# Turning the gathered rows of the experts as fp32r in place of fp32

## The reference

```python
logits = (xt @ w_router + b_router).astype(jnp.float32)
top_vals, top_idx = lax.top_k(logits, TOP_K)
top_gates = jax.nn.softmax(top_vals, axis=-1)
...
def expert_block(args):
    xb, e = args                       # up to 128 gathered tokens of expert e
    gate = xb @ w_gate[e] + b_gate[e]
    up = xb @ w_up[e] + b_up[e]
    gate = jnp.minimum(gate, SWIGLU_LIMIT)
    up = jnp.clip(up, -SWIGLU_LIMIT, SWIGLU_LIMIT)
    glu = gate * jax.nn.sigmoid(SWIGLU_ALPHA * gate)
    return (glu * (up + 1.0)) @ w_down[e] + b_down[e]
```

## Time and profile before

| | |
|---|---|
| median of 3 runs | 1856.83 us (1856.76, 1856.83, 1863.29) |
| profiled execution | 1863.21 us, span 1861.9 us |
| PE busy | 1802.1 us (97%) |
| DVE busy | 1421.6 us (76%) |
| ACT busy | 1177.9 us (63%) |
| POOL busy | 192.2 us (10%) |
| read from HBM | 481.56 MB |

### The profile page before, as it was taken

One profiled execution on the slowest core, in us unless ns is written; L12 is line 12 of the kernel. 1 busy time (PEld: TensorE's weight loads), 2 busy tenths in 40 slices (PEclk: granted clock), 3 DMA queues, 4 the chain that ended last, 5 costly groups with the idle time before them and its releaser, 6 DMA issues.

```text
span 1861.9 us, 20805 instructions
## 1 busy us (share of the span) xinstructions
PE 1802.1 (97%) x8267; PEld 1445.1 (78%) x8267; DVE 1421.6 (76%) x1219; ACT 1177.9 (63%) x879; POOL 192.2 (10%) x127
## 2 busy tenths in 40 slices
PE   7999969999999999999999999999998999999998
PEld 5777757888888888888888888888874777778876
DVE  4476569999999999999999999999895523765342
ACT  4353457777777777777777777777772346564231
POOL 1311010111211211111121121111001000000000
PEclk9999979999999999999999999999998999999999
DMA  7311339999999999999999999999995322122221
GB/s 259 114 46 68 130 142 360 368 367 364 362 379 365 359 381 361 368 363 367 365 366 371 367 360 370 365 369 369 367 360 216 136 68 68 46 73 90 94 77 45
DMA packets 95330, 487.16 MB, mean 262 GB/s; under 512 B 13864, under 2 KB 15440, under 8 KB 45312
## 3 DMA queue, kind: packets, MB, share of 16 engines
q1 hardware_dynamic: 81408, 462.64, 66.3%
q0 software_dynamic: 9520, 17.13, 2.4%
q10 hardware_dynamic: 4304, 6.03, 1.0%
HBM read 481.56 MB, written 20.97 MB: 270 GB/s over the span
## 4 chain that ended last, share of the span: by engine, by line
PE 93%; DVE 4%; ACT 2%; DMA 1%; issue 1%; SPq 0%; ACTq 0%; POOLq 0%; DVEq 0%
PE PS L445 85%; PE PS L677 3%; PE PS L849 1%; DVE WL L1229 1%; PE PS L861 1%; PE PS L842 1%; DMA ring<-in_w_in_dram 1%; ACT WH L914 1%; PE PS L477 0%; PE PS L555 0%; DVE X L1240 0%; DVE X L1552 0%; DMA xg<-h2d,tok 0%; DVE X L1555 0%; DVE HG L1559 0%
## 5 line engine op out<-in xcount | busy, mean ns | idle before, releaser
L1229 DVE TENSOR_TENSOR WL<-ring,WH 128x2048 fp32r<-128x2048 f32 x428 | 967.1, 2287 | 236.5 <-ACT WH L914 232.8
L914 ACT ACTIVATE WH<-ring 128x2048 fp32r<-128x2048 f32 x428 | 815.7, 1915 | 355.1 <-PE PS L445 350.4
L445 PE MATMUL PS<-WH,xh 128*128 128x512 f32 x1024 | 328.6, 402 | 4.1 <-ACT xh L1060 2.2
L445 PE MATMUL PS<-WL,xh 128*128 128x512 f32 x1024 | 317.6, 391 | 0.0
L445 PE MATMUL PS<-WH,xl 128*128 128x512 f32 x1024 | 274.5, 390 | 0.0
L445 PEld LDWEIGHTS PS<-WL,xh 128*128 128x128 f32 x1024 | 192.8, 188 | 41.2
L445 PEld LDWEIGHTS PS<-WH,xl 128*128 128x128 f32 x1024 | 192.7, 188 | 41.3
L445 PEld LDWEIGHTS PS<-WH,xh 128*128 128x128 f32 x1024 | 188.5, 189 | 43.5 <-ACT xh L1060 2.8
L1777 POOL DMA_INDIRECT yd<-ys,dst x32 | 74.0, 2314 | 971.2 <-ACT ys L1075 971.2
L445 PE MATMUL PS<-WH,hh 128*128 128x512 f32 x512 | 160.7, 395 | 1.1 <-ACT hh L1060 1.1
L445 PE MATMUL PS<-WL,hh 128*128 128x512 f32 x512 | 158.4, 390 | 0.0
(11 more groups left out here) (343 smaller groups left out, 2158.5 us busy)
## 6 DMA issues: line engine op xcount, KB each, us to landing
ring<-in_w_gate_dram SPq DMA_DIRECT2D x128, 1024.0 KB, 7.5
ring<-in_w_up_dram SPq DMA_DIRECT2D x128, 1024.0 KB, 7.3
ring<-in_w_down_dram SPq DMA_DIRECT2D x128, 1024.0 KB, 8.5
ring<-in_w_in_dram SPq DMA_DIRECT2D x32, 1024.0 KB, 5.4
ring<-in_w_out_dram SPq DMA_DIRECT2D x8, 1024.0 KB, 5.0
yk<-yd SPq DMA_DIRECT2D x4, 1024.0 KB, 9.3
X<-in_x_dram SPq DMA_DIRECT2D x4, 512.0 KB, 9.7
h2d<-HV ACTq DMA_DIRECT2D x4, 512.0 KB, 3.2
```

The source lines that it names most:

```text
L445: return P.matmul(ps, a, b, start=start, stop=stop)
L914: A.activation(WH[buf[n]], ring[spot[n]], ACT.Copy).then_inc(s_hi, 1)
L1229: V.tensor_tensor(WL[buf[n]], ring[spot[n]], WH[buf[n]].bitcast(F32), SUB).then_inc(s_lo, 1)
```

## The change

The two buffers xg get the type fp32r. A new tile identr of 128x128 fp32r holds the identity; DVE fills it once, by a copy of ident, in vector_routing. tensor_turn8 takes the type and the identity as arguments: for the gathered rows PE gets fp32r data, identity and output, for eu it stays fp32. GpSimd's gather and memset go to the same bytes as before through a cast of the type.

```diff
-    xg = [reg(f"xg{i}", [128, D], F32, 4 * i) for i in range(2)]
+    xg = [reg(f"xg{i}", [128, D], F32R, 4 * i) for i in range(2)]
+    identr = reg("identr", [128, 128], F32R, 49)
...
-    def tensor_turn8(src):
+    def tensor_turn8(src, dt, one):
         pairs_ = src.rearrange("t (c p k) -> t c k p", p=128, k=2)
         for k in range(8):
-            last = P.transpose(PS[:, 6 + k // 4, 128 * (k % 4):128 * (k % 4) + 128], pairs_[:, k // 2, k % 2], ident)
+            last = P.transpose(PS[:, 6 + k // 4, 128 * (k % 4):128 * (k % 4) + 128].bitcast(dt), pairs_[:, k // 2, k % 2], one)
         last.then_inc(s_tt, 1)
...
-        tensor_turn8(xg[e % 2])
+        tensor_turn8(xg[e % 2], F32R, identr)
...
-        tensor_turn8(eu.rearrange("p h f -> p (h f)"))
+        tensor_turn8(eu.rearrange("p h f -> p (h f)"), F32, ident)
...
         normed(HV[3], 3, 7, G2).then_inc(s_norm, 1)
+        V.tensor_copy(identr, ident)
         low(first + NS - 1)
...
-        G.indirect_dma_start(xg[i], None, h2d, bass.IndirectOffsetOnAxis(tok[:, e:e + 1], 0), bounds_check=T - 1,
+        G.indirect_dma_start(xg[i].bitcast(F32), None, h2d, bass.IndirectOffsetOnAxis(tok[:, e:e + 1], 0), bounds_check=T - 1,
...
-            G.memset(xg[i], 0.0).then_inc(s_mz, 1)
+            G.memset(xg[i].bitcast(F32), 0.0).then_inc(s_mz, 1)
```

## The result

The changed kernel takes 1860.54 us in the median of 22 runs (1859.45 to 1866.54), the kernel before 1857.94 us (1856.22 to 1863.29, 22 runs). The ratio is 1.0019 with a 95% interval of 1.0012 to 1.0025: slower by 3.5 us (2.2 to 4.6; the two medians alone are 2.6 us apart, and the runs of either kernel spread over 7 us). That is under the 0.5% that I had called no change, but it is clear of noise and on the other side of zero than my sum of -0.3 us. The time lies inside my range of 1851 to 1866 us, but by luck: the room above was left for the slower of two levels of the same program, not for a dearer transpose.

What follows compares the result with a forecast made beforehand. PE was taken to bound the kernel; 256 transposes at 119 against 120 ns gave -0.3 us, the other terms 0, so 1856.83 - 0.3 = 1856.5 us, with a range of 1851 to 1866 us.

Steps and rivals of the forecast that it cites:

- the room above: Upper end of the 1851 to 1866 us range, added for the upper of one program's two levels, 1856.8 and 1863.3.
- What bounds the kernel: PE sets the pace, busy 1000.00 of 1000.00 us from 300 to 1300 us; transfers follow at 367 GB/s.
- the sum for the 256 transposes: PE's turns of gathered rows: a rounded transpose costs 119 ns against 120 in fp32, together -0.3 us.
- both bounds: Limits for the 256 transposes: -2.3 us if fp32r removes the step's penalty, +1.5 us from a product batch at 126 ns.
- The lower bound from the step: Turns of xg: fp32r might remove the penalty for taking every second element, 256 x -9 = -2.3 us.
- The load rule of the Trainium skill: PE's weight loads: 107 ns for 128 columns, so at most 13 ns gained per transpose, -3.3 us, more likely nothing.
- Rival 1: Rounded transposes of gathered rows are paced by their columns, 67 ns not 120: -13.6 us, 1843.2 us; chance 11%.
- Rival 3: Each rounded transpose runs as an ordinary single precision product in two halves, 275 ns: +39.7 us, 1896.5 us; chance 6%.
- Rival 2: Transposes get faster but the weights do not follow, DMA staying at 367 GB/s: about 1856 us, no change; chance 3%.
- The copy on DVE: In the routing after HV, the 128x128 identity copy, nearest row 0.22 us, fits into a 0.89 us wait: 0.
- GpSimd's work and the remainder xl: GpSimd's memset, gather and casts move the same bytes; DVE's xl and its products keep size and time: no cost.
- The first turn: First turn of gathered rows at 250.33 us, 1.98 us at a low clock: costed at nothing, at most half given back.

Runs made afterwards that it cites:

- The probes: Kernel before plus series of 16 PE instructions behind its last product; with a step of two: fp32 transposes 115 to 120 ns, fp32r transposes 141, fp32r products 118 to 121.

## Why the prediction was wrong

**What bounds the kernel: right.** A change of a turn's price came through to the whole. The thirty turns give 0.13 us per expert and the kernel lost 3.5 us, with both turns rounded it lost twice that, and PE stayed busy for all of the 1000 us from 300 to 1300. Of the 4.0 us between my 1856.5 and the measured 1860.54, 1.1 us is only that the median of the kernel before went from 1856.83 to 1857.94 with more runs.

**The step that failed** is the sum for the 256 transposes, "119 against 120 ns, 256 x -1 = -0.3 us". The 119 ns were measured on ordinary fp32r products, and for those they are right: with the same rows and step as the change an ordinary product kept the kernel at 0.9994, and its probe gives 118 ns. I carried the number over to a transpose on the ground that the load of 128 four-byte columns sets the pace in either. That is what the runs refute: a rounded transpose costs 81 to 88 ns side by side, less than any product, and 140 with a step of two, more than any other form with that step. The transposes inside a turn went from 120 to 140 ns, and net of the earlier start of the turn (0.13 us per turn of eight) the term is 256 x about +16 ns, +4.2 us, outside both bounds (-2.3 to +1.5 us), since both bounds came from products and from fp32.

**The lower bound from the step pointed the wrong way.** I had seen that fp32 loads pay for a step (111 against 120 ns) and asked only what it would be worth if fp32r did away with it. That fp32r could pay more for it was not asked. That the time still fell inside the range of 1851 to 1866 us is luck. The step was in front of me, as xg's load row of 205 ns beside HG's of 144.

**The load rule of the Trainium skill** ("TensorE: Matmul & The Clock Gate", section on LDWEIGHTS: the columns over 1.2, with no term for the type, so 107 ns for 128) fits the fp32 transposes and fp32r products that read neighbours (109 to 113 ns). The rounded transpose differs from it both ways, 81 to 88 ns and 140, and so does the product with a step of four, 234 ns; the measurement decides.

**Rival 1** (paced by its columns, 67 ns) did not come, but its idea was half right: side by side this form does break through the 107 ns. **Rival 3** had the direction by another mechanism: there are still 256 records, none in two halves, and 1896.5 us was far off. **Rival 2** did not arise.

**The copy on DVE: right,** shown by the run that has it alone. That GpSimd's work and the remainder xl cost nothing more was not tested by itself; the experiments leave no loss over for them. **The first turn** was to cost nothing and gave 0.6 us back: a rounded transpose with a step is 140 ns from start to start at the low clock too, behind the first of the turn, where an fp32 one takes 213.

What stays open is why PE takes 140 ns for a stepped rounded transpose. The probes show that it is the step and the form together; which part of the load or of the move is slow, no run here tells. Nor does one tell whether a rounded turn keeps the low part of the rows, on which xl rests.

## What to carry to other kernels

A price belongs to the operation, the type and the pattern of its operand together; before carrying one over to a form that the trace lacks, put 16 of that form behind the last product and read start to start. Where fp32 rows have to be turned, lay them out so that the 128 elements of a transpose are neighbours and then turn them in fp32r; with a step, leave them in fp32. And put a reordering where an engine reads PSUM anyway; DVE pays for it in SBUF, reading or writing.

## What the runs showed of the hardware that was not expected

- Transposes of 128x128 from start to start, at a granted clock of 1.00: fp32 109 to 111 ns side by side and 113 to 120 with a step, fp32r 81 to 88 and 134 to 143.
- fp32r products whose loaded operand has a step: 118 to 121 ns with two elements, 234 with four, 240 with eight (this last at 0.50 alone). The series with four began at a granted clock of 1.00 and ran on after its fall without a change of pace.
- At the granted clock of 0.50 the first turn took 1.98 us in fp32 and 1.37 in fp32r with the step, 213 and 140 ns from start to start, so the 140 ns do not follow PE's clock. Side by side the fp32r turn took 1.26 us there, 127 ns where it has 82 to 86 at 1.00, and as ordinary fp32r products 1.97 us: at the low clock the step costs a rounded transpose 13 ns, at the high one more than 50.
- DVE, 128x1024 elements: with one or two operands read from SBUF with a step of 32 bytes 2.14 to 2.16 us in place of 1.22 to 1.29; with one read from PSUM with that step 1.22; with the output written with a step of 512 bytes 2.05.
